# Second feed-forward matrix by Strassen's scheme, in turn with tiles of the first, and the first of four weight sums on VectorE

## What is computed

```python
D_MODEL, SEQ, D_FF = 2048, 256, 4 * 2048
...
h = h + rms_norm(mixed, g_mix_post[l])
f = rms_norm(h, g_ffn_pre[l])
f = jnp.square(jax.nn.relu(f @ w_ff1[l])) @ w_ff2[l]
h = h + rms_norm(f, g_ffn_post[l])
```

## Time and profile before

| | |
|---|---|
| runs | 2152.02, 2152.32, 2153.08 us (median 2152.32) |
| profiled execution | span 2150.6 us, granted TensorE clock 0.999 |
| TensorE busy | 2125.1 us, 99% |
| VectorE busy | 1361.9 us, 63% |
| ScalarE busy | 1106.1 us, 51% |
| GpSimd busy | 156.2 us, 7% |
| DMA | 395.17 MB, mean 184 GB/s |
| chain that ended last | TensorE 35%, VectorE 1%, ScalarE 1% |

### The profile page before, as it was taken

The page is one execution under the profiler, slowest core; times in us unless marked ns, Lnnn a source line. Parts: engine busy times, 40 slices in busy tenths (PEclk is TensorE's granted clock), DMA queues, the critical chain, the costliest instruction groups (busy, mean ns, idle before and its releaser), DMA issues. The chain is left out here.

```text
span 2150.6 us, 29240 instructions
## 1 busy us (share of the span) xinstructions
PE 2125.1 (99%) x11602; PEld 1841.8 (86%) x11602; DVE 1361.9 (63%) x1979; ACT 1106.1 (51%) x1541; POOL 156.2 (7%) x78
## 2 busy tenths in 40 slices
PE   8999999999999999999999999999999999999998
PEld 7888888888988888888888888888888888888886
DVE  5554568875577558876578678766555555555555
ACT  4444554454464555555455455656435534544543
POOL 0000000000000000000007873000000000000000
PEclk9999999999999999999999999999999999999999
DMA  8666545655576655655656654646666666666664
GB/s 278 196 189 187 165 138 174 179 172 186 185 214 186 178 148 159 174 167 176 191 180 198 193 178 151 215 136 206 193 193 190 189 193 193 189 194 190 192 190 145
DMA packets 325031, 395.17 MB, mean 184 GB/s; under 512 B 20848, under 2 KB 252912, under 8 KB 324128
## 3 DMA queue, kind: packets, MB, share of 16 engines
q1 hardware_dynamic: 323104, 383.21, 59.0%
q0 software_dynamic: 1792, 10.10, 1.2%
HBM read 391.16 MB, written 2.10 MB: 183 GB/s over the span
## 5 line engine op out<-in xcount | busy, mean ns | idle before, releaser
L490 DVE TENSOR_TENSOR low<-raw,high 128x1024 fp32r<-128x1024 f32 (+2 forms) x672 | 809.9, 1209 | 639.0 <-ACT high L934 635.3
L934 ACT ACTIVATE high<-raw 128x1024 fp32r<-128x1024 f32 (+2 forms) x732 | 763.0, 1046 | 775.8 <-PE acc L682 201.7
L682 PE MATMUL acc<-xhl,high 128*128 128x512 f32 x3198 | 766.4, 391 | 0.0
L682 PEld LDWEIGHTS acc<-xhl,high 128*128 128x128 f32 x3198 | 587.0, 188 | 113.8 <-issue 0.7
L699 PE MATMUL acc<-xhl,low 128*128 128x256 f32 x3200 | 436.9, 286 | 1.9 <-DVE xhl L1792 1.4
L699 PEld LDWEIGHTS acc<-xhl,low 128*128 128x128 f32 x3200 | 414.4, 191 | 18.1 <-DVE xhl L1792 1.8
L686 PE MATMUL acc<-high,yhl 128*128 128x512 f32 (+1 forms) x1036 | 380.1, 373 | 2.2 <-DVE work L1718 1.6
L687 PE MATMUL acc<-high,yhl 128*128 128x512 f32 (+1 forms) x1036 | 378.8, 372 | 0.0
L702 PE MATMUL acc<-low,yhl 128*128 128x512 f32 (+1 forms) x1036 | 241.9, 374 | 0.2
L686 PEld LDWEIGHTS acc<-high,yhl 128*128 128x128 f32 x1036 | 195.2, 188 | 36.8 <-DVE work L1718 2.0
L687 PEld LDWEIGHTS acc<-high,yhl 128*128 128x128 f32 x1036 | 195.2, 188 | 33.8
(11 more groups left out here) (228 smaller groups left out, 1286.9 us busy)
## 6 DMA issues: line engine op xcount, KB each, us to landing
raw<-in_w_in SPq DMA_DIRECT2D x328, 512.0 KB, 3.7
raw<-in_w_ff SPq DMA_DIRECT2D x256, 512.0 KB, 3.9
raw<-in_w_out SPq DMA_DIRECT2D x91, 512.0 KB, 4.3
raw<-in_w_mem_kv SPq DMA_DIRECT2D x32, 512.0 KB, 5.0
raw<-in_w_in SPq DMA_DIRECT2D x16, 256.0 KB, 2.7
raw<-in_w_out SPq DMA_DIRECT2D x10, 256.0 KB, 2.8
x_nat<-in_mem SPq DMA_DIRECT2D x4, 512.0 KB, 7.8
x_nat<-in_x POOLq DMA_DIRECT2D x4, 512.0 KB, 6.4
```

The costliest lines, as they stand in the source:

```text
L490: eng.tensor_tensor(part(low, g), part(raw, g), part(high, g).bitcast(F32), ALU.subtract).then_inc(ready, 1)
L682: ins = pe.matmul(acc[:, 2 * (c.acc % 2) + s, :], wh[:, t, at], vhl, start=first, stop=last)
L934: act.activation(part(high, g), part(raw, g), ACT.Copy).then_inc(high_ready, 1)
```

## The change

The first 12 blocks (chunks ("f1", 0, 0 to 2)) stay as they are, up to their relu and square, which VectorE now does from SBUF (`first_tiles`). The rest of the feed-forward part is new:

- **Hidden tiles.** w_ff1 comes in 58 tiles of 128 hidden columns, ("g1", n), two blocks each, in rows of 512 bytes. `hidden_tile(n)` multiplies them into one bank (obank). ScalarE copies it out (`tile_copy`), VectorE adds the halves and does relu and square (`hidden_rows`). Two tiles make a pair.
- **Groups.** w_ff2 comes in 60 groups: 256 rows (a pair) by 1024 columns, 1 MB in two DMAs (`load_group`) to `bset`, two slots. Taken as 2 x 2 of [128 rows x 512 columns], a group is multiplied with the pair's 2 x 2 (two tiles of hidden columns by two halves of the tokens) in 7 products instead of 8 (Strassen's scheme in Winograd's form). That wants four sums of weights (`first_sum` on VectorE, the other three in two instructions of `group_sums` on GpSimd) and four of hidden values (`pair_sums` on GpSimd); high and low parts of 7 units of 512 weights (`split_h` on ScalarE, `split_l` on VectorE) and of 7 combinations of 128 hidden values (`pair_h`, `pair_l`). `group` on TensorE does 7 x 3 matmuls into seven banks. After four groups (four pairs) VectorE adds the seven banks to `msum` (`sums_out`), with the rest on GpSimd (`add_sums`).
- **The rest.** Rows of w_ff2 for the last four pairs, columns 1024 to 2047, are eight direct blocks (`last_block`), 12 matmuls each.
- TensorE's order is group g, then hidden tile g + 6. VectorE's step g makes first_sum and the splits of group g + 1, the hidden rows of tile g + 5 and the low parts of tile g + 6. The low part is written over raw (`raw_r`), so a slot comes free when TensorE has used it.
- The norm's factor on the hidden values (`sq3`) is no longer applied to the sums; it goes into the epsilon of the last norm (`epsv`).

The diff, cut to its core (new functions, and the queues of the engines):

```diff
-    for q in range(NQ):
...
-        for n, (col, width) in enumerate(FCOLS):
-            add(("f2", q, n), a["w_ff2_2"][0], col, width=width, row0=D * q)
+    for n in range(TILES_AHEAD, TILES):
+        add(("g1", n), w, P * n, width=P, nk=8)
+    for n in range(2, NF):
+        add(("f2", n), a["w_ff2_2"][0], CW * n, row0=P * (TILES - 8), kts=8)
...
+TILES, TILES_AHEAD = 64, 6
+GROUPS = 60
...
+            def group(g):
+                pair, _ = where(g)
+                first, last = pair % 4 == 0, pair % 4 == 3
+                pe.wait_ge(pair_ready, pair + 1)
+                hid, units = hidden(pair), bset_r[:, g % 2]
+                for n, (p, unit, combo_no) in enumerate(PRODUCTS):
+                    pe.wait_ge(split_high, 3 * g + (1, 1, 2, 2, 3, 3, 3)[n])
+                    if first:
+                        product_released(g // 4, p)
+                    for hl in range(2):
+                        pe.matmul(bank_of[p], hid[:, hl, combo_no, :], units[:, 7 + unit, :], start=first and hl == 0,
+                                  stop=False)
+                for n, (p, unit, combo_no) in enumerate(PRODUCTS):
+                    pe.wait_ge(split_low, 3 * g + (1, 1, 2, 2, 3, 3, 3)[n])
+                    ins = pe.matmul(bank_of[p], hid[:, 0, combo_no, :], units[:, unit, :], start=False, stop=last)
+                ins.then_inc(group_used, 1)
...
+            for g in range(GROUPS):
+                group(g)
+                if g + TILES_AHEAD < TILES:
+                    hidden_tile(g + TILES_AHEAD)
...
+            def hidden_rows(n):
+                t = tile_buf[n % 2]
+                dve.wait_ge(tile_out, n - TILES_AHEAD + 1)
+                link(dve.tensor_tensor(t[:, 0:S], t[:, 0:S], t[:, S:2 * S], ALU.add))
+                v = t[:, 0:S].rearrange("p (s n) -> p s n", s=ST)
+                dve.wait_ge(pair_ready, n // 2)
+                dve.scalar_tensor_tensor(out=combo[:, 1:3, :] if n % 2 else combo[:, 0:8:7, :], in0=v, scalar=0.0, in1=v,
+                                         op0=ALU.max, op1=ALU.mult).then_inc(relu_ready, 1)
...
+            def first_sum(g):
+                units = bset[:, g % 2]
+                dve.wait_ge(group_landed[g % 2][0], 16 * (g // 2 + 1))
+                if g:
+                    dve.wait_ge(sum_step, 3 * g)
+                dve.tensor_tensor(units[:, 1, :], units[:, 1, :], units[:, 0, :], ALU.subtract).then_inc(sum_step, 1)
...
+            def split_l(g, part_no):
+                dve.wait_ge(sum_step, 3 * g + 3)
+                dve.wait_ge(split_high, 3 * g + part_no + 1)
+                at, end = ((2, 4), (0, 2), (4, 7))[part_no]
+                dve.tensor_tensor(bset_r[:, g % 2, at:end, :], bset[:, g % 2, at:end, :], bset_r[:, g % 2, 7 + at:7 + end, :].bitcast(F32),
+                                  ALU.subtract).then_inc(split_low, 1)
...
+                dve.wait_ge(group_used, 4 * k + 4)
...
+                out(dve.tensor_tensor(m11, m11, bank_of[2], ALU.add))
+                out(dve.tensor_tensor(m12, m12, bank_of[3], ALU.add))
...
+            for g in range(GROUPS):
+                n, ahead = g + TILES_AHEAD - 1, g + 1 < GROUPS
+                if ahead:
+                    first_sum(g + 1)
+                if g and n < TILES:
+                    hidden_rows(n)
+                if g:
+                    low_block(FF1 + 2 * g)
+                    low_block(FF1 + 2 * g + 1)
+                if ahead:
+                    split_l(g + 1, 0)
+                    split_l(g + 1, 1)
+                if g % 4 == 3:
+                    sums_out(g // 4)
+                if ahead:
+                    split_l(g + 1, 2)
+                if g % 2 == 0 and n < TILES:
+                    pair_l(g // 2 + 2)
...
+            def load_group(g):
+                if g < 2:
+                    sp.wait_ge(xt_ready, 40)
+                else:
+                    sp.wait_ge(group_used, g - 1)
+                pair, half = where(g)
+                for t in range(2):
+                    r0, col = P * (2 * pair + t), 2 * CW * half
+                    dst = bset[:, g % 2, 2 * t:2 * t + 2, :].rearrange("p a b -> p (a b)")
+                    sp.dma_start(dst, a["w_ff2_2"][0][r0:r0 + P, col:col + 2 * CW]).then_inc(group_landed[g % 2][t], 16)
...
+            def group_sums(g):
+                units = bset[:, g % 2]
+                pool.wait_ge(group_landed[g % 2][1], 16 * (g // 2 + 1))
+                pool.wait_ge(sum_step, 3 * g + 1)
+                pool.tensor_tensor(units[:, 4, :], units[:, 3, :], units[:, 1, :], ALU.subtract).then_inc(sum_step, 1)
+                pool.wait_ge(sum_step, 3 * g + 2)
+                t2 = units[:, 4, :].unsqueeze(1).broadcast_to([P, 2, CW])
+                pool.tensor_tensor(units[:, 5:7, :], t2, units[:, 0:3:2, :], ALU.subtract).then_inc(sum_step, 1)
+            def pair_sums(pair):
+                pool.wait_ge(relu_ready, tiles_made(pair))
+                n0 = 4 * pair
+                pool.tensor_tensor(combo[:, 3, :], combo[:, 7, :], combo[:, 2, :], ALU.add).then_inc(pair_step, 1)
+                pool.tensor_tensor(combo[:, 5, :], combo[:, 0, :], combo[:, 7, :], ALU.subtract).then_inc(pair_step, 1)
+                pool.wait_ge(pair_step, n0 + 1)
+                pool.tensor_tensor(combo[:, 4, :], combo[:, 3, :], combo[:, 0, :], ALU.subtract).then_inc(pair_step, 1)
+                pool.wait_ge(pair_step, n0 + 3)
+                pool.tensor_tensor(combo[:, 6, :], combo[:, 1, :], combo[:, 4, :], ALU.subtract).then_inc(pair_step, 1)
+            def add_sums(k):
+                m = msum[:, k % 2]
+                pool.wait_ge(out_step, 7 * k + 7)
+                pool.tensor_tensor(m[:, 0, :], m[:, 0, :], flat(au[:, :, :]), ALU.add).then_inc(out_added, 1)
+                both = u3.unsqueeze(1).broadcast_to([P, 2, CW])
+                at = m[:, 1, :].rearrange("p (a b) -> p a b", a=2)
+                pool.tensor_tensor(at, at, both, ALU.add).then_inc(out_added, 1)
...
+            for g in range(GROUPS):
+                if g + 1 < GROUPS:
+                    group_sums(g + 1)
+                if g % 2 == 0 and g + TILES_AHEAD - 1 < TILES:
+                    pair_sums(g // 2 + 2)
+                if g % 4 == 0 and g:
+                    add_sums(g // 4 - 1)
```

More of the change, by code:

```diff
@@ L54 @@
 CONV_OPS = 8 * TAPS
-NQ = 4
 ALPHA = (2 * DEPTH) ** 0.25
@@ L489, in low_part, with where, used_by, hidden @@
             eng.wait_ge(high_ready, g + 1)
-            eng.tensor_tensor(part(low, g), part(raw, g), part(high, g).bitcast(F32), ALU.subtract).then_inc(ready, 1)
+            out = part(rawr if g >= FF1 else low, g)
+            eng.tensor_tensor(out, part(raw, g), part(high, g).bitcast(F32), ALU.subtract).then_inc(ready, 1)
+        def where(g):
+            e, i = divmod(g, 8)
+            return 4 * e + i % 4, i // 4
+        def used_by(pair):
+            return 8 * (pair // 4) + 4 + pair % 4
+        def hidden(pair):
+            slot = pair % 5
+            return hid4 if slot == 4 else hid03[:, slot]
+        def tiles_made(pair):
+            return pair + 1 if pair < 3 else 2 * pair - 1
+        tile_buf = [flat(cross), tile_b[:, :]]
+        def m_cols(n):
+            return msum[:, n // 2, :, CW * (n % 2):CW * (n % 2) + CW]
+        last_banks = {2: (obank[:, :], sbank[:, :]), 3: (tb[:, 0, :], tb[:, 1, :])}
+        at_a = 2 * (by["f1", 0, 2].acc % 2)
+        at_b = 2 - at_a
+        bank_of = {2: sbank[:, :], 3: tb[:, 0, :], 1: tb[:, 1, :], 5: acc[:, at_b, :], 6: acc[:, at_b + 1, :],
+                   7: acc[:, at_a, :], 4: acc[:, at_a + 1, :]}
         block = ctx.enter_context(nc.Block())
@@ L726, in weight_block, with hidden_tile, with_high, with_low @@
                     ins = with_low(g == c.blocks[-1])
+                ins.then_inc(block_used, 1)
+            def hidden_tile(n):
+                if n > TILES_AHEAD:
+                    pe.wait_ge(tile_out, n - TILES_AHEAD)
+                for i, g in enumerate(by["g1", n].blocks):
+                    wh, wl = part(high, g), part(rawr, g)
+                    def with_high():
+                        pe.wait_ge(high_ready, g + 1)
+                        for t in range(8):
+                            ins = pe.matmul(obank[:, :], wh[:, t, :], flat(xhl[:, 8 * i + t]), start=i == 0 and t == 0,
+                                            stop=i == 1 and t == 7)
+                        return ins
+                    def with_low():
+                        low_taken(pe, g)
+                        for t in range(8):
+                            ins = pe.matmul(obank[:, S:2 * S], wl[:, t, :], xh[:, 8 * i + t, :], start=False, stop=False)
+                        return ins
+                    if i:
+                        with_low()
+                        ins = with_high()
+                    else:
+                        with_high()
+                        ins = with_low()
+                    ins.then_inc(block_used, 1)
@@ new lines, in gain_sums @@
```

(40 more changed lines are left out.)

350 lines of the change are left out of this document (239 added, 111 removed).

## The result

| | before | changed |
|---|---|---|
| median of the runs | 2152.7 us (2152.0 to 2153.3, 4 runs) | 2356.4 us (2352.4 to 2356.8, 4 runs) |
| ratio | 1 | 1.0941, 95% interval 1.0926 to 1.0957 |
| span of the profiled execution | 2150.6 us | 2350.6 us |

The kernel became 9.4% slower, inside the range and 37 us under the number given. The profiled execution of the changed kernel took 2352.4 us as a whole, 4 us less than its median.

What follows compares the result with a forecast made beforehand. VectorE and GpSimd, taking turns at SBUF, were to bind the loop: 8.03 + 5.83 + 1.13 = 15.0 us a step. Loop start 1481 plus 875.5 plus an end of 34.8 gave span 2391.3, median 2393 us; 8-in-10 range 2265 to 2465.

Steps and rivals of the forecast that it cites:

- TensorE, 10.34 us a step: TensorE's work in one loop step: 21 matmuls of 0.227 us for a group plus 5.57 us for a hidden tile.
- VectorE, 9.16 us a step: VectorE's work in one loop step: 8.03 us with two SBUF inputs plus 1.13 us for sums_out from PSUM.
- GpSimd, 5.83 us a step: GpSimd's sums in one loop step, with 1.30 us for 512 elements, 2.39 for 1024 and 0.47 for 128.
- A handoff I cost at nothing: In the loop, passing work between engines adds 0 us, since overlaps and a semaphore are each about 0.1 us.
- The exclusion: In the loop, two-SBUF-input VectorE instructions and SBUF-reading GpSimd instructions shut each other out, so 8.03 and 5.83 us add.
- GpSimd has nothing ready beside sums_out: In the loop, GpSimd's next group_sums waits for a first_sum behind sums_out, so sums_out adds its 1.13 us a step.
- Start: Before the loop: the first group's sums are done at 1463.4 us and the loop begins at 1481.
- End: After the last split: 4.2 us until last_block, 21.8 for eight direct blocks, 8.8 after the last matmul; 34.8 us.
- The clock: Rival: TensorE's idling in the loop lowers its granted clock; 2729 us at the lower level throughout, some 2500 between; chance 0.06.
- DMA at nothing: Loading 2 MB a loop step costs nothing, covered by TensorE's and VectorE's work; 140 GB/s at 15 us a step.
- Partly hidden: Rival: half of GpSimd's instruction time falls into VectorE's waits and beside its PSUM instructions; 2222 us, chance 0.10.
- TensorE stays the bound: Rival: VectorE and GpSimd run side by side, so a loop step is 10.34 us; 2124 us, chance 0.06.

## Why the prediction was right, point by point

**TensorE, 10.34 us a step: right.** With GpSimd reading nothing, four steps take 1752.19 - 1710.94 = 41.25 us, 10.31 each (10.35 on average over its loop), and TensorE is busy all the time. 40.9 us were there to be had, and that kernel is 12 us faster than the one before.

**VectorE, 9.16 us a step: right.** Uncontended, every term came as read from the earlier trace rows: two low parts 2.27 from start to start (1721.51 less than 1723.78), the splits 3.93, sums_out 4.30.

**GpSimd, 5.83 us a step: its durations right, what they cost VectorE too high.** 512 elements take 1.30 us as estimated; four of 128 follow by about 0.41 us where VectorE is quiet (0.47 estimated). But what a GpSimd instruction adds to VectorE's queue is less than its duration. In the changed kernel and the one with all sums on VectorE, from start to start:

| GpSimd instruction | beside VectorE's | with it | alone | adds |
|---|---|---|---|---|
| 512 elements, 1.30 us | L2017 | 1703.78 - 1702.45 = 1.33 | 0.34 | 0.99 |
| 1024 elements, 2.40 us | L2027 | 1716.41 - 1713.20 = 3.21 | 1.01 | 2.20 |
| three of 128, 0.41 us each | splits L2042 | 1713.20 - 1708.47 = 4.73 | 3.93 | 0.27 each |

By these GpSimd adds (4 x 3.19 + 8 x 0.27 + 2 x 2.20) / 4 = 4.83 us a step, and the step is 9.16 + 4.83 = 13.99. Measured, from the first first_sum in the loop (1482.38) to the last (2292.55): 810.2 / 58 = 13.97. That close a match is in part luck: VectorE also waited 13.4 us in 14 steps for ScalarE's copy of a tile, 0.23 a step, for which the sum has no term. The forecast was 15.0. So the mis-sized term is "A handoff I cost at nothing", with its overlaps left to the range, and the 0.47 us for 128 elements, which count 0.27: the loop to its last split took 822.4 us where 875.5 stood, 53 less, 24 of them by pair_sums (120 x 0.20). The range has a slip here too: by the prediction's own rule a fixed part of 0.1 or 0.3 us moves an instruction of 512 elements by 0.05 and one of 128 by 0.09 us, 0.22 a step, so 13 us each way and not 24. And one of its signs misled: GpSimd's small instructions are listed at over 1 us, and the forecast was too high, not too low, because the listed time is mostly waiting.

The same prices give group_sums on VectorE: 3.19 - 2.05 (its two sums as followed in the timeline, 2.66 - 0.61) = 1.14 us less a step, 2289 (measured 2286). All on VectorE: 4.83 less, 2.05 + 0.57 + 0.53 more (group; output, 2 x 1.13 in four steps; pair, 1.06 in two with a wait of 0.1), 99 us less and 10.6 for landing, 2268 (2264). sums_out moved: 14 x 3.19 = 45 us less, 2312 (2312). For the pair's sums alone they give no change, and 13 us were measured (8.6 between the profiled executions, 8.1 of it in the loop). There VectorE's waits for ScalarE's copy of a tile fell from 13.4 us (14 times) to 3.6 (6 times), which is of that size; that they are the cause was not tested.

**The exclusion: right, and shown.** By the low parts' 4.77 us against 2.35, by the kernel that only writes, and by the one that works beside sums_out. One reading under it was loose: in the earlier trace rows the instruction of 1144.01 waits for GpSimd's of 1141.73, and the one with an input from PSUM runs beside GpSimd's next, of 1144.68, not under the same one. The conclusion stands.

**"GpSimd has nothing ready beside sums_out": right for this kernel,** and the price of it is measured: 44 us. It was a property of the order, not of the engines. When first_sum goes back to GpSimd, part of it vanishes too.

**Start: right.** The loop begins at 1482.38 where 1481 stood, and on the way the first group's sums are there at 1464.0 (1463.4 forecast).

**End: 11 us too short.** From the last split (2304.74) to the end it took 45.9 us where 34.8 stood. The timeline of TensorE there:

```profile
2306.01 1.22 PE L836 MATMUL sbank<-bset_r,hid 128*128 128x512 f32 x2 [7.39 <-DVE hid L2027]
2307.02 1.91 PE L836 MATMUL tb<-bset_r,hid 128*128 128x512 f32 x4
...
2311.70 1.07 PE L840 MATMUL acc<-bset_r,hid 128*128 128x512 f32 x4
2313.75 0.47 PE L868 MATMUL obank<-high,hid 128*128 128x512 f32 x1 [0.98 <-DVE msum L2059]
...
2337.95 0.39 PE L869 MATMUL tb<-high,hid 128*128 128x512 f32 x1
```

The step that failed is "pair_l with its extra part 1.2, two low parts 2.3, 0.7: 4.2 us": it has no term for the last group's own 21 matmuls. They start when pair_l is done and take 6.8 us, in part slowly (1.22 us for the first two; after 7.4 us of waiting the granted clock was 0.54 from 2306 to 2310), and the two low parts lie beside them: 9.0 us from the last split to 2313.75. The eight blocks took 24.6 us (21.8 forecast; 2.1 of the rest is a wait for a low part whose block landed late), and behind the last matmul 12.3 (8.8 forecast; why VectorE's work there is longer was not looked into).
Loop, start and end together: -53.1 + 1.4 + 11.1 = -40.6 us, and 2391.3 becomes the 2350.6 measured, up to rounding. So the number came out better than the terms: the end, too short by 11 us, hid a fifth of the loop's excess.

**The clock: right that it decides nothing.** With TensorE idle for 9.6 us in front of its first group the granted clock fell to 0.50 (1.2 GHz) and was back at 1.00 by 1490; in the loop it was 0.91 (1700 to 1900). The forecast of "busy for about two thirds" was too low: 82%. A step of 13.97 us makes 10.34 / 13.97 = 74% of it; an estimate with the lower clock, 10.34 / 0.91 / 13.97 = 81%, gives nearly all the rest. And TensorE waited for the tile's low part and the pair's, hardly for the group's splits.

**DMA at nothing: right at 14 us a step,** not quite at 12.4, where VectorE waited 10.6 us for it.

**The rivals.** "Partly hidden" (2222) needed GpSimd's work to fall beside VectorE's PSUM instructions half the time; made to do so once in four steps, it gave 44 us. "TensorE stays the bound" gave 2124; without collisions it is 2135 to 2140, that is, the sum with the end corrected by 11 us. No run shows anything for "no change".

## What to carry to other kernels

Before work is spread over VectorE and GpSimd, look at where each one's inputs lie: VectorE instructions with two SBUF inputs and GpSimd instructions that read SBUF go into one sum, and in this kernel only VectorE's instructions with an input from PSUM were cover for GpSimd. Then the order in the queues is worth as much as the split of the work: seven instructions moved from one side of the next first_sum to the other gave 44 us, and the pair's low part, moved in front of the split that had covered its wait, cost 23. A tail needs its own sum that starts with the work of the last loop step itself.
